# Inner norms of a two-layer decoder trunk: where the statistics of the last three token tiles, their square roots and the second group's evictions stand in line

## The reference

```python
def trunk(x, ...):
    for layer in range(2):
        mix = even_mixer(x) if layer == 0 else odd_mixer(x)
        x = layer_norm(alpha * x + mix, ln1_g[layer], ln1_b[layer])
        x = layer_norm(alpha * x + squared_relu_mlp(x), ln2_g[layer], ln2_b[layer])

def layer_norm(x, g, b):
    mu = mean(x); var = mean((x - mu) ** 2)
    return (x - mu) * rsqrt(var + eps) * g + b
```

## Time and profile before

| what | us |
|---|---|
| median of 3 runs | 2477.61 (2476.06 to 2480.05) |
| the profiled execution's own time | 2482.34 |
| its span, first to last instruction | 2480.5 |
| TensorE busy in it | 2395.8 |
| mean granted TensorE clock | 0.991 |

### The profile page before, as it was taken

The page is one execution under the profiler, slowest core; times in us unless marked ns, Lnnn a source line. Parts: engine busy times, 40 slices in busy tenths (PEclk is TensorE's granted clock), DMA queues, the critical chain, the costliest instruction groups (busy, mean ns, idle before and its releaser), DMA issues.

```text
span 2480.5 us, 35489 instructions
## 1 busy us (share of the span) xinstructions
PE 2395.8 (97%) x14110; PEld 2132.6 (86%) x14110; DVE 1028.9 (41%) x2084; ACT 605.8 (24%) x1280; POOL 481.2 (19%) x222
## 2 busy tenths in 40 slices
PE   8999999999999999999999888999999999999996
PEld 7888888898998998998999555688899899898895
DVE  3555666632222222226723655456622222222228
ACT  1223205220120220223300466515121121121120
POOL 2101212121121122113511100112221221121130
PEclk9999999999999999999999999999999999999998
DMA  5101321231232232232311566642242231241241
GB/s 181 61 18 35 117 67 63 74 122 66 83 111 74 84 98 82 90 101 85 115 44 68 212 230 230 255 41 74 70 128 68 75 127 62 73 135 62 73 135 72
DMA packets 69726, 245.81 MB, mean 99 GB/s; under 512 B 25584, under 2 KB 30320, under 8 KB 61040
## 3 DMA queue, kind: packets, MB, share of 16 engines
q1 hardware_dynamic: 52944, 173.68, 20.6%
q10 hardware_dynamic: 16688, 70.83, 9.5%
HBM read 230.33 MB, written 81.97 MB: 126 GB/s over the span
## 4 chain that ended last, share of the span: by engine, by line
PE 87%; DVE 7%; ACT 3%; issue 2%; DMA 1%; POOL 1%; SPq 0%; ACTq 0%; DVEq 0%
PE PS L1463 45%; PE PS L1537 34%; ACT SMB L805 1%; PE PS L1794 1%; PE PS L1768 1%; DVE XT L1133 1%; DMA WR<-in_w 1%; PE PS L1485 1%; PE PS L1807 1%; POOL WS L558 1%; PE PS L1782 1%; PE PS L1833 1%; PE PS L1582 1%; PE PS L1607 1%; DVE BNS L958 1%
## 5 line engine op out<-in xcount | busy, mean ns | idle before, releaser
L1463 PE MATMUL PS<-XS,WS 128*128 128x384 f32 (+1 forms) x7056 | 1190.7, 328 | 14.5 <-DVE XS L919 11.3
L1463 PEld LDWEIGHTS PS<-XS,WS 128*128 128x128 f32 x7056 | 1167.0, 189 | 29.4 <-issue 18.9
L558 POOL TENSOR_TENSOR WS<-WR,WS 128x1024 fp32r<-128x1024 f32 x178 | 436.8, 2454 | 1825.8 <-DVE WS L934 1054.7
L1537 PE MATMUL PS<-WS,HID 128*128 128x512 f32 x3072 | 703.7, 389 | 0.0
L1537 PEld LDWEIGHTS PS<-WS,HID 128*128 128x128 f32 x3072 | 575.7, 188 | 119.1 <-issue 0.5
L1133 DVE TENSOR_TENSOR XT<-XT,PS 128x512 f32<-128x512 f32 x360 | 236.9, 686 | 372.7 <-PE PS L1537 372.5
L760 ACT ACTIVATE RT<-PS 128x384 f32<-128x384 f32 (+1 forms) x192 | 91.2, 475 | 1098.5 <-PE PS L1463 1098.5
L1212 DVE TENSOR_TENSOR HID<-ST,HID 128x384 fp32r<-128x384 f32 (+1 forms) x192 | 108.4, 564 | 578.5 <-ACT HID L766 578.5
L1537 PE MATMUL PS<-WS,XS 128*128 128x512 f32 x768 | 179.9, 393 | 4.2 <-DVE XT L1133 4.0
L1537 PEld LDWEIGHTS PS<-WS,XS 128*128 128x128 f32 x768 | 144.3, 189 | 35.3 <-DVE XT L1133 5.0
L934 DVE CAST WS<-WR 128x1024 fp32r<-128x1024 f32 x112 | 82.5, 738 | 107.6 <-DMA WR<-in_w 57.8
(11 more groups left out here) (182 smaller groups left out, 1356.0 us busy)
## 6 DMA issues: line engine op xcount, KB each, us to landing
WR<-in_w SPq DMA_DIRECT2D x178, 512.0 KB, 3.5
out_d_ks<-in_cache_d_k ACTq DMA_DIRECT2D x96, 340.0 KB
out_d_vs<-in_cache_d_v ACTq DMA_DIRECT2D x96, 340.0 KB
KC<-in_kt SPq DMA_DIRECT2D x16, 1024.0 KB, 10.7
VCD<-in_cache_d_v SPq DMA_DIRECT2D x16, 1024.0 KB, 6.9
TG<-in_rows SPq DMA_DIRECT2D x10, 512.0 KB, 5.7
XT<-in_xt SPq DMA_DIRECT2D x4, 1024.0 KB, 8.3
TH<-in_th SPq DMA_DIRECT2D x4, 1024.0 KB, 11.0
```

What stands on the lines that cost most here:

```text
L558: pool.tensor_tensor(WS[:, slot, 1, :], WR[:, raw, :], WS[:, slot, 0, :].bitcast(F32), ALU.subtract).then_inc(w_split, 1)
L1463: last = pe.matmul(out[:, 0:gw], WS[:, slot, a, (off + k) * P:(off + k + 1) * P], src[:, b, k, c0:c0 + gw], start=(n == 0), stop=(n == 3 * ...
L1537: last = pe.matmul(bank(b), rows, WS[:, (t0 + k) % NSLOT, f, 512 * n:512 * n + 512], start=(k == 0 and i == 0), stop=(k == 3 and i == len( ...
```

## The change

Five edits. All three inner norms are touched; norm 3 keeps its order.

1. ScalarE: root 6 leaves `ln_super` and comes at v = 0 behind the evictions of chunks 0 and 1. Scale 6 comes at v = 1, root 7 at v = 3, scale 7 at v = 4, root 8 at v = 5, scale 8 at v = 6, each behind the evictions of that v.
2. VectorE's weave: the statistics of steps 6, 7 and 8 come at v = 0, 3 and 5, behind the casts and low parts of that v.
3. VectorE's `norm_super`: the last four sums come ahead of the weight casts t0+2 and t0+3.
4. VectorE's `norm_super` no longer does step 6 in the inner norms.
5. TensorE ahead of the odd projection: unit 0 waits for the first of the last four sums alone, unit 1 for the second.

```diff
-LN_AT = {0: 7, 2: 8}
+LN_AT = {0: 6, 3: 7, 5: 8}
+ROOT_AT, SCALE_AT = {0: 6, 3: 7, 5: 8}, {1: 6, 4: 7, 6: 8}
...
                 ln_scale(l, 5)
-                ln_root(l, 6)
...
                 if v in BACK_AT:
                     ln_back(l, *BACK_AT[v])
-                if v in (0, 1, 3):
-                    ln_scale(l, 6 + (0, 1, 3).index(v))
-                if v in (0, 2):
-                    ln_root(l, 7 + v // 2)
+                if v in ROOT_AT:
+                    ln_root(l, ROOT_AT[v])
+                if v in SCALE_AT:
+                    ln_scale(l, SCALE_AT[v])
...
             def ln_weave(l, v):
-                if v in LN_AT:
-                    ln_stats(l, LN_AT[v])
                 if v in BACK_AT and high_by_vector(l, BACK_AT[v][0]):
...
+                if v in LN_AT:
+                    ln_stats(l, LN_AT[v])
...
+                sums(base, R, 4)
                 if t0 is not None:
                     freed(3 * R, 2)
                     w_high(t0 + 2)
-                sums(base, R, 4)
-                if t0 is not None:
                     w_high(t0 + 3)
-                for p in range(6, 7 if l < 3 else 9):
-                    ln_stats(l, p)
+                else:
+                    for p in range(6, 9):
+                        ln_stats(l, p)
...
-            pe.wait_ge(r_evac, ROW_BASE[10])
+            pe.wait_ge(r_evac, ROW_BASE[10] - 3)
...
+                        if woven and n == 1:
+                            pe.wait_ge(r_evac, ROW_BASE[10] - 2)
```

## The result

The changed kernel takes 2490.77 us in the median (2487.76 to 2492.27), the kernel before, beside it on the same chip, 2478.14 us: a ratio of 1.0048 with an interval of 1.0037 to 1.006. It is slower by 12.6 us; 2490 us had been forecast, with 2481 to 2498 as the range.

The account below looks back on a forecast made before the run. TensorE, busy 97% of the span, was taken as the bound; norm 0 +5.8, norm 2 +6.5 and norm 1 -0.2 sum to +12.1 us, 2489.7 us on the median, so 2490 us was forecast, range 2481 to 2498 us.

Parts of the forecast that it names:

- Part 1: Norms 0 and 2, chunks 0 and 1 evicted before root 6: waits merge into one before chunk 4, +0.1 and +0.8 us.
- clock, longer behind that wait: Norms 0 and 2: the single 4.5 us wait before chunk 4 holds TensorE's clock down longer, +0.7 us each.
- Part 2: Norms 0 and 2: third group's first transpose waits for scale 8, ending at 14.4 against 11.1 us, +3.3 us each.
- clock behind the third group's wait: Norms 0 and 2: the 3.3 us wait brings a stretch at the lower clock, +1.7 us each.
- Part 3: Norm 1, earlier sums: the 2.47 us start wait goes but VectorE falls behind, net -0.2 us, bounds -2.3 and +1.5.
- rival (c): Norms: waits move but the clock doesn't fall for them, +7.3 us, 2485 us; an edge of the forecast's 0.80 chance.
- Rival (d): All three norms: a longer stay at the low clock, +19 us, 2497 us; an edge of the forecast's 0.80 chance.
- rival (b): Third group's transposes don't wait, scale 8 ending within 11.1 us of unit 1's end: -13 us, 2465 us; chance 0.07.

Follow-up runs that it names:

- second profile of before: The kernel before, not edited, executed with a profile a second time: 2479.46 us.
- third experiment: Changed kernel with the cast of weight t0+3 in norms 0 and 2 moved behind the casts and low parts of chunks 0 and 1: 2486.76 us, 1.0033.
- second experiment: Changed kernel with statistics, roots and scales of steps 7 and 8 moved to earlier places, step 6 left behind the evictions: 2480.89 us, 1.0011.
- filled kernel: Changed kernel with 25 unused matmuls in front of chunk 4 and 18 in front of the third group in norms 0 and 2: 2488.27 us, 1.0039.
- kernels with fills: Changed kernel with unused matmuls in norms 0 and 2, in front of chunk 4 and the third group (2488.27 us) or the third group alone (2491.51 us).
- kernel without waits: Changed kernel with weight cast t0+3 later in norms 0 and 2, steps 7 and 8 early, and norm 1's own tables with scale before root: 2468.31 us, 0.9957.
- first experiment: Kernel before with only the last four sums ahead of the weight casts and norm 1's unit 0 not waiting for all: 2483.83 us, 1.0019.

## Why the prediction was right

Point by point, all in us, norm 0 and then norm 2; the measured column is from the shift of the same matmul against the profile of before (set to 0 at the norm's first transposes): at chunk 4's transposes +0.16 and +0.82, at the third group's +3.99 and +4.27, behind the norm +6.50 and +5.79. Of the second shift 3.31 and 3.30 are the third group's wait itself.

```
                                        predicted          measured
Part 1, chunk 4 starts later            0.1    0.8       0.16   0.82
clock, longer behind that wait          0.7    0.7       0.5    0.2
Part 2, third group's wait              3.3    3.3       3.31   3.30
clock behind the third group's wait     1.7    1.7       2.5    1.5
sum of the norm                         5.8    6.5       6.50   5.79
norm 1                                     -0.2             -0.60
all                                       +12.1             +11.7
```

Held against the second profile of before, the same sum is +11.7 us too, but its parts are norm 0 +8.0, norm 1 -2.0 and norm 2 +5.7. So the sum is firm, and a single norm is known to about 1.5 us.

**Part 1** held in place, and its mechanism in the main. There is no wait in front of chunk 2, there is one of 4.5 us in front of chunk 4, and GpSimd's low part goes between VectorE's two casts as assumed. The Trainium skill's page "SBUF — State Buffer", section "Who interferes with whom", was cited for the lock; the row that was missing, who goes when both stand ready, is now there: GpSimd's waiting operation ran beside VectorE's first cast, and the second ended 0.2 us behind it. The third experiment shows that GpSimd's operation is the cause: with the cast elsewhere, 2.1 us of the wait go.

The sizes +0.1 and +0.8 us came out partly by luck. The prediction had the cast of t0+3 unchanged and the later cast of t0+2 free of cost. But the sums ahead of it make GpSimd's low part of t0+2 later as well, and that stretched the cast of t0+3, in norm 0 from 0.69 to 1.46 us and in norm 2 to 1.42 us:

```profile
1698.01 1.42 DVE L929 CAST WS<-WR 128x1024 fp32r<-128x1024 f32 x1 [1.58 <-DMA WR<-in_w]
1699.35 2.80 DVE L942 CAST XS<-XR 128x384 fp32r<-128x384 f32 x2
```
```profile
1696.50 2.38 POOL L559 TENSOR_TENSOR WS<-WR,WS 128x1024 fp32r<-128x1024 f32 x1 [1.91 <-DVE WS L929]
```

In norm 0 the weight had landed 0.8 us earlier, counted from the norm's first transposes, so that the cast ended where the prediction had it. In norm 2 it had not, and these 0.7 us are the measured +0.8 us. The prediction took the 0.7 us for chunk 1's cast missing its place; it did not miss it, since the two casts take 2.80 us as in norm 0.

**Part 2** carried the forecast, and its chain of times came out to 0.1 us at each step (8.3, 11.1, 14.4). The second experiment, which undoes it alone, brings norm 0 back to -0.02 us and norm 2 to +0.59 us.

**The clock** fell behind both waits in both profiles of the changed kernel, as counted, and rival (c) is out for the norms: filling the waits takes 4.3 us from norm 0. But it is not a fixed price for each wait, as the prediction counts it: behind one of the eight third-group waits it did not fall, and the kernel before pays about 1.5 us or nothing in norm 0, depending on which of its two waits it falls behind. The term was sized as 2.4 us for each norm on top of what the kernel before paid; by the filled kernel it was 4.3 - 1.6 = 2.7 us in norm 0 and 1.3 to 2.2 us in norm 2. In norm 0 its two halves were off in opposite directions, since the longer first wait cost less than taken and the third group's more. Rival (d), a longer stay at half clock everywhere, asked for 19 us in the norms, against 11.7 and 12.6; rival (b) fell with the third group's wait, at the point named for it: scale 8 was over at 14.4 us, not within 11.1. What the experiments did not show is that a kernel gets these microseconds back in its median: both kernels with fills were as slow as, or nearly as slow as, the changed one.

**Part 3** held too. The start's wait is gone, the two small ones have come in front of units 5 and 6, and the net is -0.60 us, inside the bounds of -2.3 and +1.5 us. That a net of this size differs from none isn't shown: it is -2.0 us against the second profile of before, and the three profiles of kernels with fills, whose norm 1 is the same, have +0.05, -0.60 and +0.03 us. Compared from the norm's start, which lies 3.31 us later in the changed kernel's trace (1175.83 - 1172.52, where the earlier trace rows put the end of the work ahead), the eviction of unit 4 begins at 1211.52 - 3.31 = 1208.2, predicted 1208.7. VectorE:

```profile
1207.89 1.89 DVE L988 SCALAR_TENSOR_TENSOR XT<-XT,TG 128x1024 f32<-128x1024 f32 x1
1209.82 1.77 DVE L992 TENSOR_TENSOR XT<-XT,TG 128x1024 f32<-128x1024 f32 x1
1211.52 0.60 DVE L1268 TENSOR_SCALAR Y<-PS,COLS 128x384 f32<-128x384 f32 x1
```

The residuals in front of it are stretched from 1.22 us to 1.8, which the prediction had as waits for GpSimd's operations.

**What stays open.** The lengths of the norms are explained; the clock in stages that the change doesn't touch is not. The second layer's attention was within 0.15 us of before in both profiles of the changed kernel, but +3.75 us in the kernel without waits, +2.24 and +3.72 us in kernels with fills, and +4.93 and +1.86 us in the one with the sums alone, each time with more of it at half clock. The stages ahead of norm 0 scatter as much: 6 us between the two profiles of the kernel with both waits filled. Part of this comes and goes between executions of one kernel. Whether an edit far ahead also shifts how often it comes, as the median of the first experiment suggests (5.7 us over before, of which its norms have 1.05), no run here settles.

## What to carry to other kernels

Slack in front of a stage isn't free to spend because it looks large: here 7 us of it were taken up by two statistics, two scales and two hidden units that stood in one line on two engines, and the line was 3.3 us too long; count the whole chain to the consumer, not the moved operations alone. When a wait is taken from one place, look at what releases the next place that waits for the same engine: here two waits of 2 us became one of 4.5 us for nothing, and the kernel that gains 10 us puts the weight cast and root 6 behind the work that chunk 4 waits for, and the last statistics and scales earlier than the third group needs them. Compare the start of the same instruction in two traces, stage by stage, before believing that a difference in the total belongs to the edit; and do it in two profiles of each kernel, since a single norm moved by 1.5 us between two executions of the kernel before.

## What the runs showed of the hardware

- Two casts of VectorE that take 0.62 us together took 2.80 us when a two-input operation of GpSimd began 0.16 us into the first: the first took 0.35 us, the second 2.53 us and ended 0.2 us behind GpSimd's operation. And a weight cast of 0.69 us took 1.46 us (from 399.67) beside the end of GpSimd's operation before (398.20 to 400.58).
- Executions of one kernel differ by several microseconds through the granted clock in stages with identical code: the kernel with filled waits took 2481.68 and 2490.51 us in its two profiled executions, with the lengths equal to 0.03 us in norms 0 and 2, the stages ahead of norm 0 at half clock for nothing and for 13.6 us, and the second layer's attention at a clock of 0.98 and 0.96.
- TensorE's clock fell to half behind seven of eight idle waits of 3.0 to 3.3 us at the third group, and behind none of the six that unused matmuls filled (1.00 in both norms with both waits filled); but the medians of the kernels that had them, 2488.27 and 2491.51 us, did not show the gain against 2490.77 us of the changed kernel that the norms did.
